# A hybrid encoder block: x tiles 4 to 7 and all latents turned by VectorE blocks and DRAM scratches, in place of TensorE transposes

## The reference, cut to what matters

```
h = rmsnorm(x, norm_mix)
proj = h @ w_in          # qa, ka, va, ga, cq (384), ckv (256), kr (32), gb
ya = window_attention(qa, ka, va, sink) * silu(ga)
q = rmsnorm(cq, q_a_norm) @ w_uq          # 8 heads x (64 + 32)
kv = rmsnorm(ckv, kv_a_norm) @ w_ukv      # 8 heads x (64 + 64)
yb = latent_attention(q_nope, rope(q_rope), k_nope, rope(kr), v) * silu(gb)
out = rmsnorm(x + concat(ya, yb) @ w_out, final_norm)
```

## Time and profile before

| | |
|---|---|
| device time, median of 3 runs | 622.58 us (621.88 to 623.28) |
| span of the profiled execution | 621.7 us |
| the profiled execution's own time | none printed beside the span; the three runs lie 0.2 to 1.6 us above it |
| TensorE busy | 612.4 us, 99% |
| VectorE, ScalarE, GpSimd busy | 71%, 58%, 51% |
| DMA, mean | 124 GB/s |

### The profile page before, as it was taken

One profiled execution on the slowest core, in us unless ns is written; L12 is line 12 of the kernel. 1 busy time (PEld: TensorE's weight loads), 2 busy tenths in 40 slices (PEclk: granted clock), 3 DMA queues, 4 the chain that ended last, 5 costly groups with the idle time before them and its releaser, 6 DMA issues.

```text
span 621.7 us, 9412 instructions
## 1 busy us (share of the span) xinstructions
PE 612.4 (99%) x3252; PEld 501.4 (81%) x3252; DVE 440.0 (71%) x853; ACT 358.8 (58%) x770; POOL 318.3 (51%) x303
## 2 busy tenths in 40 slices
PE   7999999999999999999999999999999999999996
PEld 6888898888888888888887777777777777888885
DVE  5774327333544428988999788989988898789684
ACT  6662223123334227877786777788787778633563
POOL 4625004403656542536547777887788789510701
PEclk9999999999999999999999999999999999999999
DMA  7540007375685820101015723223323423499043
GB/s 223 204 162 1 0 24 248 117 267 181 221 275 196 262 64 14 34 2 35 1 27 130 217 70 92 62 59 89 90 61 76 103 85 137 140 334 370 1 149 122
DMA packets 49934, 76.90 MB, mean 124 GB/s; under 512 B 5656, under 2 KB 25632, under 8 KB 49760
## 3 DMA queue, kind: packets, MB, share of 16 engines
q1 hardware_dynamic: 49728, 76.04, 39.4%
q10 hardware_dynamic: 160, 0.27, 0.1%
HBM read 46.54 MB, written 20.05 MB: 107 GB/s over the span
## 4 chain that ended last, share of the span: by engine, by line
PE 95%; DVE 2%; DMA 1%; ACT 1%; POOL 1%; issue 0%; SPq 0%; ACTq 0%
PE ps L1565 18%; PE ps L1567 18%; PE ps L1566 18%; PE ps L1858 10%; PE ps L1876 5%; PE ps L1875 5%; PE ps L1790 5%; PE ps L1795 5%; PE ps L1760 3%; PE ps L1810 2%; PE ps L1770 2%; PE ps L1747 2%; PE ps L1746 1%; PE ps L1771 1%; PE ps L1577 1%; DMA wn_raw<-w_in 1%
## 5 line engine op out<-in xcount | busy, mean ns | idle before, releaser
L1419 DVE TENSOR_TENSOR pT_lo<-ps,pT_hi 128x512 fp32r<-128x512 f32 x128 | 88.2, 691 | 16.8 <-ACT pT_hi L1032 16.8
L1032 ACT ACTIVATE pT_hi<-ps 128x512 fp32r<-128x512 f32 x128 | 76.1, 597 | 37.0 <-PE ps L1858 36.8
L744 POOL TENSOR_SCALAR p_b<-p_b,stat 128x1024 f32<-128x1024 f32 x64 | 72.0, 1125 | 37.0 <-DVE stat L1414 36.9
L1565 PE MATMUL ps<-hT_hi,w_hi 128*128 128x512 f32 x208 | 84.0, 404 | 0.0
L1567 PE MATMUL ps<-hT_hi,w_lo 128*128 128x512 f32 x208 | 81.3, 391 | 0.0
L1566 PE MATMUL ps<-hT_lo,w_hi 128*128 128x512 f32 x208 | 81.1, 390 | 0.0
L1858 PE MATMUL ps<-ident,p_b 128*128 128x128 f32 x512 | 78.1, 275 | 0.2 <-DVE pT_lo L1419 0.2
L1409 DVE TENSOR_REDUCE stat<-ps 128x1 f32<-128x1024 f32 x64 | 77.7, 1215 | 0.7 <-PE ps L1810 0.6
L1858 PEld LDWEIGHTS ps<-ident,p_b 128*128 128x128 f32 x512 | 60.8, 140 | 21.2 <-issue 7.7
L1021 ACT ACTIVATE p_b<-ps,stat 128x1024 f32<-128x1024 f32 x64 | 71.3, 1114 | 6.5 <-DVE stat L1409 4.0
L1875 PE MATMUL ps<-pT_hi,vB 128*128 128x512 f32 x128 | 55.4, 433 | 0.0
(11 more groups left out here) (217 smaller groups left out, 1479.3 us busy)
## 6 DMA issues: line engine op xcount, KB each, us to landing
w_raw<-w_in SPq DMA_DIRECT2D x13, 512.0 KB, 4.7
x_in<-x SPq DMA_DIRECT2D x8, 512.0 KB, 3.8
wt_raw<-w_out SPq DMA_DIRECT2D x8, 512.0 KB, 4.5
t_scratch<-wt_hi SPq DMA_DIRECT2D x16, 256.0 KB, 2.6
t_scratch<-wt_lo SPq DMA_DIRECT2D x16, 256.0 KB, 2.6
q<-q_h SPq DMA_DIRECT2D x16, 256.0 KB, 3.6
wn_raw<-w_in SPq DMA_DIRECT2D x8, 336.0 KB, 3.7
k<-k SPq DMA_DIRECT2D x9, 256.0 KB, 2.9
```

The costliest lines, as they stand in the source:

```text
L744: nc.gpsimd.tensor_scalar(p_b[:, (U + 1) % 4, :], p_b[:, (U + 1) % 4, :], r_b[:, U % 4:U % 4 + 1], 0.5, ALU.mult, ALU.mult).then_inc(s_bp, 1)
L1032: nc.scalar.activation(pT_hi[:, 1 - G % 2, 4 * a:4 * a + 4, U % 4 * P:(U % 4 + 1) * P], ps[:, 4 + a, :].rearrange("p (k c) -> p k c", c=P) ...
L1419: nc.vector.tensor_tensor(pT_lo[at_], ps[:, 4 + a, :].rearrange("p (k c) -> p k c", c=P), f(pT_hi[at_]), ALU.subtract).then_inc(s_bTl, 1)
L1565: nc.tensor.matmul(o, a_hi, b_hi, start=first, stop=False, skip_group_check=goes_on)
```

## The change

Tiles 0 to 3 of x are turned by TensorE as before. For tiles 4 to 7 (X_PE = 4), VectorE turns the 32x32 blocks of x_n into x_blk, of which there is one; four DMAs (32 partitions each) store x_blk to a DRAM scratch, with the blocks put where the full transpose has them, and one DMA fetches the tile back into the rows of latT_hi or latT_lo, which are unused then. `h_hi` and `h_lo` read it from there. The latents of all eight tiles go the same way through lat_b and a second scratch, back into lat (`move_lat`). The orders of ScalarE, VectorE and SyncE are changed with it, both kr jobs stand behind the first r jobs, and lat_b shares bytes with kr_r and kr_t. The diff, cut to its core:

```
@@ UP @@
-            UP += [("q", j, half) for j in range(4)] + [("r", 0, half), ("r", 1, half), ("kr", 0, half)]
+            UP += [("q", j, half) for j in range(4)] + [("r", 0, half), ("r", 1, half)]
+            if half == 0:
+                UP += [("kr", 0, i) for i in range(2)]
@@ SyncE @@
+            def store_x(t):
+                sp.wait_ge(s_xblk, t - X_PE + 1)
+                for q in range(4):
+                    sp.dma_start(xt_scr[t - X_PE, :, :, q, :].rearrange("a p c -> p a c"),
+                                 x_blk[q * Q32:(q + 1) * Q32].rearrange("p a k c -> p a (k c)")).then_inc(s_xsto, 16)
+            def fetch_x(t):
+                sp.wait_ge(s_xsto, 64 * (t - X_PE + 1))
+                if t >= X_PE + 2:
+                    sp.wait_ge(s_hhi, 2 * (t - 1))
+                sp.dma_start(x_turned(t), xt_scr[t - X_PE].rearrange("a p (r q) c -> (a p) r (q c)", r=2)) \
+                    .then_inc(s_xq[t % 2], 16)
             load_x(6)
+            store_x(4)
             load_x(7)
+            for t in range(X_PE, NT - 1):
+                fetch_x(t)
+                store_x(t + 1)
+            fetch_x(NT - 1)
             ...
             (uq_raw load)
+            def move_lat(t):
+                sp.wait_ge(s_lblk, t + 1)
+                for q in range(4):
+                    sp.dma_start(lt_scr[t, :, :, q, :].rearrange("a p c -> p a c"),
+                                 lat_b[q * Q32:(q + 1) * Q32].rearrange("p a k c -> p a (k c)")).then_inc(s_lout, 16)
+                sp.wait_ge(s_lout, 64 * (t + 1))
+                sp.dma_start(lat[:, t % 2, :], lt_scr[t].rearrange("a p q c -> (a p) (q c)")).then_inc(s_lin[t % 2], 16)
+            for t in range(NT - 1):
+                move_lat(t)
             sp.wait_ge(s_pB, NT)
             (ukv_raw and r_q loads)
+            move_lat(NT - 1)
@@ GpSimd @@
             pool.wait_ge(s_uqi, 16)
-            pool.wait_ge(s_xT, 2 * NT)
+            pool.wait_ge(s_xblk, NT - X_PE)
@@ ScalarE @@
             def h_hi(t, halves=range(2)):
+                if t >= X_PE:
+                    act.wait_ge(s_xq[t % 2], 16 * (1 + (t - X_PE) // 2))
+                    for r in range(2):
+                        nc.scalar.activation(h_cols(hT_hi, t, r), x_quads(t, r), ACT.Copy).then_inc(s_hhi, 1)
+                    return
             (square_x)
+                if t >= X_PE + 2:
+                    act.wait_ge(s_xblk, t - 1 - X_PE)
+                elif t >= 2:
             def lat_hi(t):
-                act.wait_ge(s_lT, t + 1)
-                (two activations from PSUM)
+                act.wait_ge(s_lin[t % 2], 16 * (t // 2 + 1))
+                nc.scalar.activation(lat_cols(latT_hi, t), lat_quads(t), ACT.Copy).then_inc(s_lhi, 1)
             (lat_stats: squares of tiles 2 to 7 go to PSUM banks 0 and 1, no wait for s_lT)
             square_x(5)
-            h_hi(4)
             wn_hi_k(7)
             square_x(6)
+            h_hi(4)
+            square_x(7)
             h_hi(5)
-            square_x(7)
             lat_stats(0)
             ...
             for j, (kind, t, h) in enumerate(UP):
+                if j == 4:
+                    lat_hi(NT - 1)
@@ VectorE @@
             (lat_norm)
+                dve.wait_ge(s_lat, t + 1)
+                if t >= 1:
+                    dve.wait_ge(s_lout, 64 * t)
+                nc.vector.transpose(lat_b[:, :, :, :],
+                                    lat[:, t % 2, :].rearrange("p (k a c) -> p a k c", a=4, c=Q32)).then_inc(s_lblk, 1)
+            def turn_blocks(t):
+                dve.wait_ge(s_xn, 2 * (t + 1))
+                if t > X_PE:
+                    dve.wait_ge(s_xsto, 64 * (t - X_PE))
+                nc.vector.transpose(x_blk[:, :, :, :],
+                                    x_n[:, t % 2, :].rearrange("p (k a c) -> p a k c", a=4, c=Q32)).then_inc(s_xblk, 1)
+            for t in range(X_PE, NT):
                 norm_x(t)
-                if t < NT - 1:
-                    h_lo(t - 1)
+                turn_blocks(t)
+                if t == X_PE:
+                    h_lo(X_PE - 1)
+            h_lo(4)
+            h_lo(5)
             lat_norm(0)
             h_lo(NT - 2)
             h_lo(NT - 1)
             for t in range(1, NT):
                 lat_norm(t)
-            lat_lo(NT - 2)
-            lat_lo(NT - 1)
             dve.wait_ge(s_rnat, 16)
+            dve.wait_ge(s_lout, 64 * NT)
             (kr_t and kr_r)
+            lat_lo(NT - 2)
+            lat_lo(NT - 1)
@@ TensorE @@
-            (turn_lat, and turn_x(4), turn_x(5), turn_x(6), turn_x(7), turn_lat(0) to turn_lat(7))
                 if j == 0:
+                    pe.wait_ge(s_lat, 6)
                     pe.wait_ge(s_latT, 4)
                     pe.wait_ge(s_uq, 1)
-                elif j == 2:
-                    pe.wait_ge(s_lat, 7)
-                if j == 6:
+                elif j in (2, 4):
+                    pe.wait_ge(s_lat, 6 + j // 2)
+                if j == 8:
                     pe.wait_ge(s_latT, NT)
```

More of the change, by code:

```diff
@@ L50 @@
 LT = QLT + KVLT
+Q32 = 32
 A_SCALE = HD ** -0.5
@@ L63 @@
 BASE = 16512
+X_PE = 4
 ACT_UNITS = range(2, 16, 2)
@@ L80, in encoder @@
     v_scr = nc.dram_tensor("v_scratch", [SEQ, HEADS * HD], F32, kind="Internal").ap()
+    xt_scr = nc.dram_tensor("x_turned_scratch", [NT - X_PE, 4, Q32, 4, KT * Q32], F32, kind="Internal").ap()
+    lt_scr = nc.dram_tensor("lat_scratch", [NT, 4, Q32, 4, LT * Q32], F32, kind="Internal").ap()
     with ExitStack() as ctx:
@@ L107, in encoder @@
         lat = at("lat", 147, [P, 2, QL + KVL])
+        lat_b = at("lat_b", 153, [P, 4, LT, Q32])
         kr_n = at("kr_n", 152, [P, NT, ROPE])
@@ L114, in encoder @@
         latT_lo = at("latT_lo", 185, [P, LT, SEQ], F32R)
+        x_blk = at("x_blk", 161, [P, 4, KT, Q32])
         uq_raw = at("uq_raw", 115, [P, QLT, HEADS, QK])
@@ L220, in encoder @@
         s_xT, s_hhi, s_hT = sem("xT_done"), sem("hT_hi_ready"), sem("hT_ready")
+        s_xblk, s_xsto = sem("x_blocks_turned"), sem("x_blocks_stored")
+        s_xq = [sem(f"x_turned_in{i}") for i in range(2)]
         s_wnh, s_wnr = sem("wn_hi_ready"), sem("wn_ready")
@@ L225, in encoder @@
             "va_hi_ready", "lat_ssq_ready", "lat_var_ready", "lat_rms_ready", "lat_ready"))
-        s_lT, s_lhi, s_latT = sem("lat_transposed"), sem("latT_hi_ready"), sem("latT_ready")
+        s_lblk, s_lout, s_lhi, s_latT = (sem(n) for n in (
+            "lat_blocks_turned", "lat_blocks_stored", "latT_hi_ready", "latT_ready"))
+        s_lin = [sem(f"latT_in{i}") for i in range(2)]
         s_krr = sem("k_rope_ready")
@@ L345, in encoder, with lat_quads, lat_cols, x_turned @@
         B_GROUPS = B_UNITS // 4
+        def lat_quads(t):
+            return lat[:, t % 2, :].rearrange("p (q k c) -> p k q c", q=4, c=Q32)
+        def lat_cols(a, t):
+            return a[:, :, t * P:(t + 1) * P].rearrange("p k (q c) -> p k q c", c=Q32)
+        def x_turned(t):
+            a, r = ((latT_hi, 0), (latT_hi, 2), (latT_lo, 0), (latT_lo, 2))[t - X_PE]
+            return f(a[:, r:r + 2, HALF:SEQ])
+        def x_quads(t, r):
+            return x_turned(t)[:, r, :].rearrange("p (q k c) -> p k q c", q=2, c=Q32)
+        def h_cols(a, t, r):
+            c = t * P + r * 2 * Q32
+            return a[:, :, c:c + 2 * Q32].rearrange("p k (q c) -> p k q c", c=Q32)
         def nat_banks(t):
@@ L821, in square_x @@
                 act.wait_ge(s_x[t % 2], 16 * (t // 2 + 1))
-                if t >= 2:
+                if t >= X_PE + 2:
+                    act.wait_ge(s_xblk, t - 1 - X_PE)
+                elif t >= 2:
                     act.wait_ge(s_xT, 2 * (t - 1))
@@ L853, in lat_stats @@
                                      ACT.Copy)
-                if t >= 2:
-                    act.wait_ge(s_lT, t - 1)
-                nc.scalar.activation(lat[:, t % 2, 0:QL], ps[:, a, P:NA], ACT.Square,
+                if t == 2:
+                    act.wait_ge(s_hT, 2 * NT)
+                squares = lat[:, t, :] if t < 2 else ps[:, 0:2, :].rearrange("p b c -> p (b c)")
+                nc.scalar.activation(squares[:, 0:QL], ps[:, a, P:NA], ACT.Square,
                                      accum_out=lss[:, 0:1]).then_inc(s_va, 1)
@@ L859, in lat_stats @@
                 nc.scalar.activation(kr_n[:, t, :], ps[:, b, KVL:KVL + ROPE], ACT.Copy)
-                nc.scalar.activation(lat[:, t % 2, QL:QL + KVL], ps[:, b, 0:KVL], ACT.Square,
-                                     accum_out=lss[:, 1:2]).then_inc(s_lss, 1)
+                nc.scalar.activation(squares[:, HALF:HALF + KVL] if t >= 2 else squares[:, QL:QL + KVL],
+                                     ps[:, b, 0:KVL], ACT.Square, accum_out=lss[:, 1:2]).then_inc(s_lss, 1)
                 if t >= 2:
@@ L899, in _ @@
             lat_hi(NT - 2)
-            lat_hi(NT - 1)
             for j, (kind, t, h) in enumerate(UP):
+                if j == 4:
+                    lat_hi(NT - 1)
                 if kind in BY_DVE:
```

(32 more changed lines are left out.)

## The result

The changed kernel takes 635.71 us (median of 4 runs, 634.3 to 637.0), the kernel before 622.5 us in the same comparison (621.88 to 623.28): ratio 1.0213, 95% interval 1.0198 to 1.0227. It is 13.2 us slower. I had predicted 629.9 us, with a range of 624 to 637.

The account below looks back on a forecast made before the run. TensorE, busy 99% of the span and 95% of the chain, was taken to bound the kernel. 12.5 + 1.7 + 1.0 - 7.9 = +7.3 us on a span of 621.7 gave 629.0, or 629.9 us as a time; range 624 to 637.

Parts of the forecast that it names:

- What goes away: TensorE drops 32 transposes of x and 40 of latents, 0.109 us each by the chain: 7.9 us saved.
- rival of full-duration transposes: On TensorE, each dropped transpose is worth its 275 ns: 15.2 - 19.8 = -4.6, 618 us; chance 0.03.
- The pause before natural(3): TensorE idles 12.5 us for s_lat 1, which stands behind block turns and three store round trips in series.
- Quick stores: Store 4 isn't held up by the queue and TensorE's pace doesn't fall: +1.0 to +3.6, 624 to 626 us; chance 0.18.
- faster than before: Block turns so cheap that round trips nearly vanish, idle time before natural(3) under 6.9 us: -1.3, 621.3 us; chance 0.06.
- The slow pace: Behind the wait before natural(3), TensorE starts at a slower pace after idling: 1.7 us lost, bounds 0 to 1.9.
- Tile 4, uq_raw, latent turns within tiles: No wait at tile 4 (1.5 us of margin); late uq_raw and seven of eight latent turns hidden behind TensorE's work.
- The last latent: In the up jobs TensorE waits 0.4 us for s_krr and 0.6 us for lat_lo: together 1.0 us, bounds 0 and 4.
- slow transfers: Round trips before natural(3) take 6.5 us, idle 17 us, tile 4's margin goes: +11 to +17, 634 to 640 us; chance 0.10.

Follow-up runs that it names:

- e10: Kernel with all x by TensorE, latents by blocks, lat_b apart and r_q loaded behind the last latent, but tile 7's latent turned by TensorE: 618.81 us, ratio 0.9947.
- e4: Changed kernel plus 115 unused transposes of the identity on TensorE in its pause before natural(3, 0): 633.75 us, ratio 1.0178.
- e7: e1_x_only with latents 0 to 2 normalized between the block turns, and h_lo(4) and h_lo(5) behind turns 6 and 7: 621.91 us, ratio 1.0000.
- e5_lat_apart: Changed kernel with all x turned by TensorE again, only latents by blocks, and lat_b in bytes of its own: 621.27 us, ratio 0.9986.
- e8_all: Changed kernel with e7's order, lat_b apart, r_q loaded last and early latents' transfers interleaved with those of x: 622.50 us, ratio 1.0000.
- e1_x_only: Changed kernel with the latents given back to TensorE, only x tiles 4 to 7 by blocks and DRAM: 634.48 us, ratio 1.0197.
- e9: e8_all with tile 7's latent turned by TensorE, and lat_stats(0) and lat_norm(0) ahead of square_x(6) and norm_x(6): 617.63 us, ratio 0.9925.

## Why the prediction was right in its sign and low in its size

**What goes away: right.** 7.9 us by the chain. e10 gains 3.2 us where 35 transposes at 0.109 us say 3.8 and at their duration of 0.275 us 9.6; the rival of full-duration transposes falls.

**The pause before natural(3): right in its steps, 1.1 us too short.** Block turns took 1.245 us (I took 1.25) and began at 26.6, 35.4, 41.2 and 47.4 where I had 27.7, 36.6, 41.7 and 46.9. Store 4 did queue behind the load of tile 6: 5.35 us from its last issue to landing, 3.1 for the next ones. s_lat 1 was due at 52.8 and came at 52.8. That the last date agrees is luck. All engines were 1.1 us earlier in this execution, TensorE at the pause (39.3 instead of 43.04 - 2.61 = 40.4) as well as VectorE at turn 4: most of that the profiled execution of before had lost in its first 12 us, where TensorE waited 3.2 us against 2.3, and I had taken its dates as the kernel's. Against it, the two round trips of tiles 5 and 6 took 5.8 and 6.1 us where I had 5.1 and 5.2: their stores landed 3.1 and 3.0 us after the last issue, and I had taken 2.3 from the rows of other stores. That makes 1.6 us, what follows turn 7 was 0.5 us shorter, and so TensorE idled 13.6 us, not 12.5. "Quick stores" and "faster than before" both needed short trips and fall with it.

**The slow pace: right.** 1.7 us taken, 1.8 us in the trace, 2.0 us by e4.

**Tile 4, uq_raw, latent turns within tiles: right.** TensorE waits for nothing between 53 and 110 us.

**The last latent: the term that was mis-sized.** I had E + 12.8 for s_krr and 1.0 us of wait. With E = 98.5, the stores landed at E + 9.7 instead of E + 8.7, so kr_r was there at E + 14.0, and the waits were 1.7 + 0.4 = 2.1 us. And I had not carried my own term for the clock over to it: 2.1 us of waiting around 1.05 us of small transposes let the clock fall again, 1.8 us more. The term is 3.9 us, just inside the bound of 4 that I gave it.

**Sum.** 13.6 + 1.8 + 3.9 - 7.9 = 11.4; less the 1.1 us that TensorE was ahead in this execution gives 10.3. The last matmul of TensorE starts at 626.02 us against 615.83 before: 10.2 us. The tail behind it is 0.9 us longer (span 632.8 against 621.7), and that makes the 11.1 us between the two profiled executions. The tail is the landing of the last store, before and after:

```profile
out<-acc_b ACTq DMA_DIRECT2D x1, 256.0 KB, 2.7
out<-acc_b ACTq DMA_DIRECT2D x1, 256.0 KB, 3.6
```

It is 3.6 us in e4_spin too and 2.7 us in the nine other experiments, five of which have x by blocks, so nothing ties it to the change. The medians lie 13.2 us apart: the profiled execution of after was 1.1 us faster than its median, and that of before, if its time lies 1.8 us above its span too, 1.0 us slower than its own. My forecast of 7.3 us was 5.9 us too low. The terms explain 4.1 of it: 1.1 for the pause, 0.1 for the pace, 2.9 for the last latent. The other 1.8 us stay open. The four executions of the changed kernel fall into two pairs, 634.3 and 634.6, 636.8 and 637.0, all at a granted clock of 0.984 over the span, and only one of the first pair has a trace. The time ended in the bracket of my "slow transfers" rival, but not by it: its round trips of 6.5 us were 5.8 and 6.1, and its second wait at tile 4 didn't come.

What my account missed as an explanation is what e7 showed. I had written that tile 3 waits through three round trips; it waited through an order. With the same trips and another order, 12.6 us of the loss go.

## What to carry to other kernels

When work moves off the bottleneck engine onto a slower path, look at what is written behind the wait on that path and doesn't need it: putting the small thing that the bottleneck engine waits for (here 1.9 us of latent norm) ahead of it was worth 12.6 us, where a second buffer was worth 2.6 us. Leave the last item of a moved series on the old path, since nothing hides its latency: five transposes of 0.55 us in all took the place of 3.1 us of wait and 1.6 us of slow clock. And price the clock behind each wait of TensorE, not only behind the long one: here 2.1 us of waits were enough for it, in many executions.

## What the runs showed of the hardware that I had not expected

- The clock fell after short waits, and not each time. The granted clock of an execution's whole span tells it: in e5_lat_apart, with a wait of 2.1 us ahead of latT_lo, the profiled run had 0.995 and the slow pace, and was the slowest of ten (622.69 us), while eight others had 0.998 to 1.000 (one of these took 622.65 us all the same, so the clock isn't all that spreads the times). In e8_all, with 3.1 us, ten of eleven had 0.994 to 0.996. The changed kernel had 0.984 in all four, e1_x_only, without the second wait, 0.987 or 0.988. Waits of 0.7 and 1.1 us in e9 and of 1.5 and 2.1 us in the profiled run of e7 left it at 1.00; but another execution of e9, its slowest, had 0.995 over the span and has no trace. What decides in between stays open.
- In e4_spin the second pause (1.6 and 0.4 us of waits) left the clock at 1.00 in the profiled run, where the same waits lowered it in the changed kernel; the other three runs had 0.994 or 0.995.
- A block turn of 128x1024 took 1.245 us and one of 128x640 0.85 us. A reduction over 128x1024 took 1.22 us: that the blocks are turned costs VectorE next to nothing extra.
- Four stores of 128 KB from 32 partitions each landed a median 3.1 us after issue and the 512 KB fetches 4.3 to 4.4 us, so a tile's way through DRAM took about 9 us from the block turn's end: 1.4 us of issues, 3.1, and 4.3.
